# Mean squares of the next head's queries and keys: from a full-precision product between two pieces to two single-pass products inside a piece

## What is computed

```
def rmsnorm(x, g):
    xf = x.astype(F32)
    xf = xf * lax.rsqrt(jnp.mean(xf * xf, axis=-1, keepdims=True) + EPS)
    return xf.astype(x.dtype) * g
...
    qa = rope(rmsnorm(qa.reshape(b, t, A_HEADS, 2, A_DH), p['q_norm_g']), pos)
    ka = rope(rmsnorm(ka.reshape(b, t, A_HEADS, 2, A_DH), p['k_norm_g']), pos)
```

## Time and profile before

| | us |
|---|---|
| median of 3 runs | 2321.89 |
| lowest and highest | 2320.79, 2323.82 |
| span of the profiled execution, first to last instruction | 2317.6 |
| PE busy in it | 2283.8 |
| DVE, ACT, POOL busy in it | 1433.6, 1046.8, 805.3 |
| recurrent part of head 0, near matmuls of block 0 to block 6 | 37.80 |

### The profile page before, as it was taken

One profiled execution on the slowest core, in us unless ns is written; L12 is line 12 of the kernel. 1 busy time (PEld: TensorE's weight loads), 2 busy tenths in 40 slices (PEclk: granted clock), 3 DMA queues, 4 the chain that ended last, 5 costly groups with the idle time before them and its releaser, 6 DMA issues. The chain is left out here.

```text
span 2317.6 us, 46133 instructions
## 1 busy us (share of the span) xinstructions
PE 2283.8 (99%) x18425; PEld 2153.4 (93%) x18425; DVE 1433.6 (62%) x2594; ACT 1046.8 (45%) x2114; POOL 805.3 (35%) x1019
## 2 busy tenths in 40 slices
PE   7999999999999999999999999999999999999999
PEld 5898989989898989899888999999999999999999
DVE  5667676777676776765787324337546545555557
ACT  6656656556566656564333321125333333332331
POOL 1143342626252434424444124442222323222222
PEclk9999999999999999999999999999999999999999
DMA  7213121222312131211899413111111111111113
GB/s 299 92 47 103 41 87 59 73 77 57 102 54 95 49 101 49 92 46 53 326 346 347 159 61 104 46 48 51 46 46 46 46 46 46 54 43 51 46 46 99
DMA packets 75057, 213.19 MB, mean 92 GB/s; under 512 B 15579, under 2 KB 23643, under 8 KB 74843
## 3 DMA queue, kind: packets, MB, share of 16 engines
q1 hardware_dynamic: 73690, 206.05, 26.6%
q10 hardware_dynamic: 1152, 4.19, 0.4%
HBM read 175.49 MB, written 26.26 MB: 87 GB/s over the span
## 5 line engine op out<-in xcount | busy, mean ns | idle before, releaser
L170 PE MATMUL h_G<-xn_hi,h_w_hi 128*128 128x344 f32 x1368 | 457.7, 335 | 0.2 <-ACT h_d_oraw L897 0.2
L170 PE MATMUL h_G<-xn_hi,h_w_lo 128*128 128x344 f32 x1368 | 437.1, 319 | 0.0
L170 PE MATMUL h_G<-xn_lo,h_w_hi 128*128 128x344 f32 x1368 | 436.5, 319 | 0.0
L2419 POOL TENSOR_TENSOR h_w_lo<-h_w_raw,h_w_hi 128x1024 fp32r<-128x1024 f32 x87 | 215.7, 2480 | 488.8 <-DVE f_y L2620 208.7
L2341 PE MATMUL t_ps<-hn_hi,h_w_hi 128*128 128x344 f32 x1024 | 327.7, 320 | 0.9 <-issue 0.9
L2341 PE MATMUL t_ps<-hn_lo,h_w_hi 128*128 128x344 f32 x1024 | 327.1, 319 | 0.0
L2341 PE MATMUL t_ps<-hn_hi,h_w_lo 128*128 128x344 f32 x1024 | 327.0, 319 | 0.0
L1167 POOL TENSOR_TENSOR h_w_lo<-h_w_raw,h_w_hi 128x1024 fp32r<-128x1024 f32 x58 | 149.2, 2572 | 432.6 <-ACT h_w_hi L764 365.0
L170 PEld LDWEIGHTS h_G<-xn_hi,h_w_hi 128*128 128x128 f32 x1368 | 258.4, 189 | 32.5 <-issue 21.5
L170 PEld LDWEIGHTS h_G<-xn_lo,h_w_hi 128*128 128x128 f32 x1368 | 257.1, 188 | 4.4 <-issue 0.2
L170 PEld LDWEIGHTS h_G<-xn_hi,h_w_lo 128*128 128x128 f32 x1368 | 257.1, 188 | 0.0
(11 more groups left out here) (403 smaller groups left out, 5510.3 us busy)
## 6 DMA issues: line engine op xcount, KB each, us to landing
h_w_raw<-in_w_in SPq DMA_DIRECT2D x72, 512.0 KB, 3.8
h_w_raw<-in_w_ffn SPq DMA_DIRECT2D x66, 512.0 KB, 3.6
h_d_ada_w<-in_w_ada SPq DMA_DIRECT2D x32, 512.0 KB, 4.3
g_kp<-in_cache_k SPq DMA_DIRECT2D x32, 512.0 KB, 7.1
g_vp<-in_cache_v SPq DMA_DIRECT2D x32, 512.0 KB, 5.6
h_w_raw<-in_w_mix SPq DMA_DIRECT2D x24, 512.0 KB, 3.6
x<-in_xT SPq DMA_DIRECT2D x16, 516.0 KB, 7.5
n_ada_w<-in_w_ada SPq DMA_DIRECT2D x16, 512.0 KB, 13.8
```

Of the source, the lines that this page charges most:

```text
L170: ins = eng.matmul(out, w[:, k * P:(k + 1) * P], x[:, k, columns], start=(k == 0 and n == 0), stop=(k == n_k - 1 and n == 2))
L2419: pool.tensor_tensor(wlo[buf(n)][:, :], raw[n % 2][:, :], whi[buf(n)][:, :].bitcast(F32), ALU.subtract).then_inc(w_lo.sem, 1)
```

## The change

The squares of a query or key piece are split as the weights are. ACT writes the high part `sq_hi` in fp32r after it has read the piece; POOL writes the low part `sq_lo` as the difference. `blk`, which holds 1/64 and 0 and is copied once into an fp32r tile `c["blk"]`, is multiplied with each of them in a single-pass matmul, both into the same bank. The two matmuls no longer stand ahead of the piece but inside it, ahead of its fourth step (`SUMS_AT = 3`), after nine of its 24 matmuls. The low part of u = 0 is on POOL's queue behind the weight split of piece 12, those of u = 1 to 5 behind the cosine products of u = 0 to 4.

```
-def product(eng, out, whi, wlo, xhi, xlo, n_k, columns):
+def product(eng, out, whi, wlo, xhi, xlo, n_k, columns, between=None):
     for k in range(n_k):
+        if between is not None and k == between[0]:
+            between[1](*between[2])
...
+        mem = Memory(nc, "h_sq", R3, R3 + 2 * ROW)
+        sq_hi, sq_lo = ([mem(f"{n}{i}", [P, TH], F32R) for i in range(2)] for n in ("high", "low"))
...
                     qk_piece(gq if kind == "q" else gk, bank, sq[u % 2][:, :], rg[u % 2][:, :])
+                    act.wait_ge(qk_squared.sem, qk_squared.at(h, u + 1))
+                    act.activation(sq_hi[u % 2][:, :], sq[u % 2][:, :], ACT.Copy).then_inc(sq_high.sem, 1)
...
-            def qk_sums(u):
-                pe.matmul(X[:, u, 0:TH], blk[:, :], sq[u][:, :], start=True, stop=True).then_inc(qk_summed.sem, 1)
-
+            def qk_sums(h, u):
+                pe.wait_ge(sq_high.sem, sq_high.at(h, u + 1))
+                pe.wait_ge(sq_low.sem, sq_low.at(h, u + 1))
+                if u == 0:
+                    pe.wait_ge(blk_ready.sem, 1)
+                if u >= 2:
+                    pe.wait_ge(qk_ready.sem, qk_ready.at(h, u - 1))
+                pe.matmul(X[:, u % 2, 0:TH], c["blk"][:, :], sq_hi[u % 2][:, :], start=True, stop=False)
+                pe.matmul(X[:, u % 2, 0:TH], c["blk"][:, :], sq_lo[u % 2][:, :], start=False, stop=True).then_inc(qk_summed.sem, 1)
...
-                    if k < 6 and not no_next(h):
-                        pe.wait_ge(qk_squared.sem, qk_squared.at(h, k + 1))
-                        if k >= 2:
-                            pe.wait_ge(qk_ready.sem, qk_ready.at(h, k - 1))
-                        qk_sums(k % 2)
                     for n in REC_PIECES[k]:
-                        piece(h, n)
+                        piece(h, n, (SUMS_AT, qk_sums, (h, k)) if k < 6 and not no_next(h) else None)
...
+            def low_squares(h, u):
+                pool.wait_ge(sq_high.sem, sq_high.at(h, u + 1))
+                pool.tensor_tensor(sq_lo[u % 2][:, :], sq[u % 2][:, :], sq_hi[u % 2][:, :].bitcast(F32), ALU.subtract)\
+                    .then_inc(sq_low.sem, 1)
+
...
                 split_next(h, FILL_PIECE)
+                if not no_next(h):
+                    low_squares(h, 0)
...
                         pool.tensor_tensor(rg[k % 2][:, :], rg[k % 2][:, :], cos[:, cols(k % NP)], ALU.mult).then_inc(qk_cos.sem, 1)
+                        if k < 5:
+                            low_squares(h, k + 1)
...
+            copy(dve, c["blk"][:, :], blk[:, :]).then_inc(blk_ready.sem, 1)
```

More of the change, by code:

```diff
@@ L508 @@
 SQUARES_AT = (2, 4)
+SUMS_AT = 3
 def level_view(ap, lv):
@@ L596, in heads_stage @@
         qk_squared = S("qk_squared", 6, pre=6)
+        blk_ready, sq_high, sq_low = S("blk_ready", 0), S("sq_high", 6), S("sq_low", 6)
         qk_summed = S("qk_summed", 6, pre=6)
@@ L1004, in _, with piece @@
             late_value(2)
-            def piece(h, n):
+            def piece(h, n, between=None):
                 t, j = PIECES[n]
@@ L1013, in piece @@
                 w = SLOT[t]
-                ins = product(pe, G[:, n % 2, 0:TH], whi[w], wlo[w], xh, xl, KT, cols(j))
+                ins = product(pe, G[:, n % 2, 0:TH], whi[w], wlo[w], xh, xl, KT, cols(j), between)
                 if n - 1 in ADA_AT:
@@ L2678, in program @@
              pages=keep("pages", [1, NS * PAGES], I32))
+    c["blk"] = keep("blk", [P, P], F32R)
     for n in ("q", "k", "v", "qh", "kk", "f", "ib", "og", "oa", "ob"):
```

## The result

The changed kernel takes 2333.53 us, the kernel before 2321.97 (medians of 4 runs each): 1.0052 times as long, 95% interval 1.004 to 1.0065, or 11.6 us more. The forecast was 2329.6 us, slower by 7.7. The profiled span grew by 13.8 us, from 2317.6 to 2331.4; the median lies 2.1 us over the span here and 4.3 us over it before, so some 2 us of that difference are scatter between single executions. (One of the twelve executions of the kernel with half of the low part, further down, took 5684 us and is left out of its ratio.)

A forecast was written before the change was run, and what follows sets the result against it. PE looked 99% busy, but DVE's chain arrives just as PE does, so PE's gain is lost in waits. Seven heads longer by 1.1 us add 7.7 to 2321.9: 2329.6 us; own range 2326 to 2333, full range 2318 to 2335.

The forecast's parts named there:

- What bounds the kernel: Whole kernel: PE is busy 2283.8 of 2317.6 us, but DVE's operand chain arrives at the same moment as PE.
- the small row of waits on DVE: Head 0's recurrent part before the change: 11 waits of block-opening matmuls for DVE's operands, 3.4 us together.
- A sum costs PE 0.31 instead of 0.58 us: Each moved sum: two matmuls of 0.157 us replace the full-precision product; PE gains 0.27 us, 11.3 over 42 sums.
- The first wait: First piece of each head's recurrent part: PE waits some 0.87 us for POOL's low part, queued behind the weight split.
- Near(2) later by 1.0 us: Start of block 2 in a head's recurrent part: DVE's chain to it was to be longer by 1.0 us.
- its old delay: POOL's cosine product for the first rotary multiply: its old 0.2 us delay from DVE was to be missed.
- The hold of the rotary addition: Before block 2: POOL's subtraction for piece 1 was to hold DVE's rotary addition for 0.6 us.
- Pairs keep their length: From block 2 on: pairs of blocks take 12.65 us against 12.60 and 12.62, PE's gain lost waiting for DVE.
- blocks 6 and 7 have no sum, PE's queue sets their pace as before, and the 1.1 us stay in the time: Last two blocks of each head's recurrent part: pace unchanged, so the head's 1.1 us delay remains, 7.7 us over seven.
- rival C: Subtraction takes over 1.1 us, so PE waits inside later pieces too: +1.9 us per head, 2335 us; chance 0.10.
- Rival B: No lock between subtraction and rotary operations; POOL's queueing stays: 0.3 us less per head, 2319.8 us; chance 0.18.

## Why the prediction was right, and where it fell short

- **What bounds the kernel.** Right: 99% busy was not the whole truth, and the small row of waits on DVE was the one that counted. PE's busy time fell by 7 us and the span still grew by 14.
- **A sum costs PE 0.31 instead of 0.58 us.** Right, measured at 0.157 us a matmul when it does not wait (0.23 for the first matmul of the sum in block 1).
- **The first wait, 0.87 us.** Right: 0.85, which is also what its own times give (158.35 - 157.50). The subtraction took 0.92 as taken, on 157.64 to 158.56.
- **Near(2) later by 1.0 us.** 13.73 us after near(0) instead of 12.58: 1.15. The steps were those named, and the rotary multiply moved by 0.30 where 0.33 was said; but the cosine product did not miss its old delay, it took 1.12 us again. The hold of the rotary addition was forecast at 0.6 and was 0.78, the subtraction starting with the addition and not just ahead of it.
- **Pairs keep their length.** 12.92 and 12.21 us where 12.65 each was said; the sum of both, 25.13, is 0.2 under the forecast 25.3, and near(6) comes at 38.86 instead of 38.9. That the stretch agrees to a tenth is the luck of errors that cancel. Of u = 0 to 4 four rotary operations were held (1.30, 1.23, 1.25 and 1.12 us); for u = 4 none was: the subtraction came up while the addition ran and it was POOL that waited (1.27 us).
- **The failed term: "blocks 6 and 7 have no sum, PE's queue sets their pace as before, and the 1.1 us stay in the time".** They did not: the pace of block 6 was set by DVE, held by POOL. DVE's product had become 0.6 to 0.8 us later against near(6), while the weight split, which follows ACT and through it PE, kept its 3.34 us behind near(6). The product had begun half a microsecond ahead of the split before; now it began behind it and was held for 1.9 to 2.2 us: 0.8 us more in six of seven heads, 4.7 us. The stretches, forecast at 7.7 us, give 7.2 us, these 4.7 more make 12, and with the split held the kernel takes 2328.42, close to the forecast 2329.6. The time of 2333.53 lies just outside the forecast's own range of 2326 to 2333 and near rival C's 2335, but not by C's mechanism: the subtraction took over 1.1 us only where POOL was the one held, and PE waited inside a piece behind block 0 in one head alone (0.37 us). The right way to price it was in the rows of before: list every long operation of POOL (2.4 us and more, seven a head) and see what DVE does beside it once the chain has moved by 1 us.
- **The reasons.** The contention is real and follows the subtraction's length, and near(2) shows it as the larger part of the delay there, as forecast. But the lock is not the only way to lose: with the subtractions held behind the addition no rotary operation is held and the kernel is no faster, since PE now waits for the low part in front of the sum. The working had that wait for the first sum of a head only. How the 0.9 us a stretch of POOL's part divide over lock and queue in the later blocks stays open, since no run takes away the one and leaves the other, and the runs that moved operations behind the addition paid 0.11 to 0.21 us per block for the signal. Rival B had a gain of 0.3 us a head without the lock; no run shows one.

## What to carry to other kernels

When an engine is 99% busy, look for the one small wait it still has and follow the chain behind it; if that chain arrives just in time, shortening the busy engine's queue can buy nothing, and work "hidden" on the others can lengthen the chain. Before adding an operation to POOL, list which of DVE's operations on SBUF will run beside it and beside every long POOL operation after it, with all starts moved by the delay that you expect. Here a cheaper form of the data, made by the engine that writes it anyway, beat a split that costs a second operation on that engine and one on another; its price is the rounding.

## What the hardware showed that I had not expected

- An increment of a semaphore as an instruction of its own on DVE, between two dependent operations, added 0.21 us behind the addition of u = 0 (0.76 against 0.55 us from start to start) and 0.11 us for u = 1 to 5 (0.66).
- A DVE product of 128x128 in SBUF was held for 1.89 us by a POOL subtraction of 128x1024 that had started 0.36 us earlier; the hold ended some 0.15 us ahead of the subtraction's recorded end, as with the short one (0.78 of 0.93 us). Operations of DVE with one of their two inputs in PSUM were not held: `LQ` and `LK` took 1.08 to 1.09 us in all blocks, beside running POOL operations too, and the product with the reciprocal root 0.51 to 0.52.
- Single-pass matmuls that go to another bank, put in the middle of an accumulation, cost nothing beyond their own 0.157 us, except in block 1, where the second started 0.23 us after the first.
